# Two levels of the chunked attention in one burst of strip matmuls, with the queries of every other level copied by GpSimd

## The reference

```python
proj = h @ w_in
u, q, zf, zb, iv, g = jnp.split(proj, cuts, axis=-1)
k = (1.0 - lb) * jax.nn.sigmoid(-z)                  # for zf and zb
logf = jnp.logaddexp(jnp.log(lb), jnp.log1p(-lb) + jax.nn.log_sigmoid(z))
...
def step(state, inp):                                # one chunk
    b = jnp.cumsum(gb, axis=2)
    decay = jnp.exp(jnp.where(causal_in_chunk, b_t - b_s, -jnp.inf))
    scores = jnp.einsum("bhtd,bhsd,bhtsd->bhts", qb, kb, decay)
    o = einsum("bhts,bhsv->bhtv", scores, vb) + einsum("bhtd,bhdv->bhtv", qb * exp(b), state)
    state = exp(b_last)[..., None] * state + einsum("bhsd,bhsv->bhdv", kb * exp(b_last - b), vb)
...
y_rec = rms_norm(o_fwd + o_bwd, out_norm) * silu(g)
out = concat([y_fourier, y_rec]) @ w_out             # then experts: router, 16 experts, norm
```

## Time and profile before

| what | value |
|---|---|
| median of 3 runs (lowest, highest) | 2554.42 us (2551.23, 2557.26) |
| the profiled execution's own time | 2552.32 us |
| its span, first to last instruction | 2550.6 us |
| PE busy, share of the span | 98% |
| DVE, ACT, POOL busy | 65%, 53%, 13% |
| granted TensorE clock, mean | 0.997 |
| strips of line 851 | 96 bursts, 32 records each |

### The profile page before, as it was taken

One profiled execution on the slowest core, in us unless ns is written; L12 is line 12 of the kernel. 1 busy time (PEld: TensorE's weight loads), 2 busy tenths in 40 slices (PEclk: granted clock), 3 DMA queues, 4 the chain that ended last, 5 costly groups with the idle time before them and its releaser, 6 DMA issues.

```text
span 2550.6 us, 44352 instructions
## 1 busy us (share of the span) xinstructions
PE 2510.8 (98%) x18109; PEld 2263.5 (89%) x18109; DVE 1648.6 (65%) x1997; ACT 1359.3 (53%) x1627; POOL 327.1 (13%) x237
## 2 busy tenths in 40 slices
PE   7999999999999999999999999999999999999998
PEld 6777778787877999999999999999999999999997
DVE  6556565444387676767667676766767666676667
ACT  6435353434665555555555555555555555555556
POOL 3102020101120011020211202021020202102020
PEclk9999999999999999999999999999999999999999
DMA  4001010135447676675767767676676767667677
GB/s 159 26 22 55 2 55 10 57 137 198 173 144 273 231 256 239 228 261 211 268 228 251 247 235 251 226 259 234 251 249 235 248 221 256 236 234 258 225 259 282
DMA packets 63987, 503.08 MB, mean 197 GB/s; under 512 B 7536, under 2 KB 7920, under 8 KB 39568
## 3 DMA queue, kind: packets, MB, share of 16 engines
q1 hardware_dynamic: 48016, 448.84, 48.3%
q0 software_dynamic: 15872, 52.83, 7.0%
HBM read 464.42 MB, written 37.22 MB: 197 GB/s over the span
## 4 chain that ended last, share of the span: by engine, by line
PE 92%; DVE 3%; ACT 2%; DMA 1%; issue 1%; POOL 0%; SPq 0%; DVEq 0%; ACTq 0%; POOLq 0%
PE up_banks_b L2241 15%; PE up_banks_a L2241 15%; PE up_banks_b L2244 6%; PE up_banks_a L2244 6%; PE bank L64 5%; PE bank L66 5%; PE bank L65 5%; PE up_banks_b L2282 2%; PE up_banks_b L2280 2%; PE up_banks_b L2281 2%; PE up_banks_b L2279 2%; PE up_banks_a L2283 2%; PE up_banks_b L2283 2%; PE up_banks_a L2279 2%; PE up_banks_a L2282 2%; PE up_banks_a L2280 2%
## 5 line engine op out<-in xcount | busy, mean ns | idle before, releaser
L2009 DVE TENSOR_TENSOR big_lo<-wide,big_hi 128x4096 fp32r<-128x4096 f32 x189 | 836.3, 4425 | 410.2 <-ACT big_hi L1774 410.0
L1774 ACT CAST big_hi<-wide 128x4096 fp32r<-128x4096 f32 x190 | 690.3, 3633 | 515.8 <-PE up_banks_a L2241 240.8
L2241 PE MATMUL up_banks_b<-x_parts,big_hi 128*128 128x384 f32 x2016 | 574.3, 356 | 0.0
L2241 PE MATMUL up_banks_a<-x_parts,big_hi 128*128 128x384 f32 x1984 | 565.0, 356 | 1.0 <-DVE h_parts L2033 1.0
L2244 PE MATMUL up_banks_b<-x_parts,big_lo 128*128 128x192 f32 x1764 | 442.0, 251 | 0.0
L2244 PE MATMUL up_banks_a<-x_parts,big_lo 128*128 128x192 f32 x1736 | 435.0, 251 | 0.0
L2241 PEld LDWEIGHTS up_banks_b<-x_parts,big_hi 128*128 128x128 f32 x2016 | 365.3, 189 | 0.2
L2241 PEld LDWEIGHTS up_banks_a<-x_parts,big_hi 128*128 128x128 f32 x1984 | 359.4, 189 | 1.9 <-DVE h_parts L2033 1.2
L2244 PEld LDWEIGHTS up_banks_b<-x_parts,big_lo 128*128 128x128 f32 x1764 | 336.1, 191 | 0.0
L2244 PEld LDWEIGHTS up_banks_a<-x_parts,big_lo 128*128 128x128 f32 x1736 | 330.8, 191 | 0.6
L64 PE MATMUL bank<-big_hi,w_hi 128*128 128x512 f32 x576 | 236.5, 411 | 0.0
(11 more groups left out here) (345 smaller groups left out, 4177.9 us busy)
## 6 DMA issues: line engine op xcount, KB each, us to landing
wide<-in_expert_weights SPq DMA_DIRECT2D x190, 2048.0 KB, 7.7
w_raw<-in_w_heads SPq DMA_DIRECT2D x48, 256.0 KB, 2.8
x_in<-in_x SPq DMA_DIRECT2D x12, 512.0 KB, 4.0
x_d<-in_x POOLq DMA_DIRECT2D x12, 512.0 KB, 5.8
residual<-x_d POOLq DMA_DIRECT2D x12, 512.0 KB, 3.6
ffn_in<-h_and_xT_d POOLq DMA_DIRECT2D x12, 512.0 KB, 3.0
wide<-residual SPq DMA_DIRECT2D x12, 512.0 KB, 6.4
tab<-in_tables POOLq DMA_DIRECT2D x10, 512.0 KB, 7.3
```

The costliest lines, as they stand in the source:

```text
L1774: nc.scalar.copy(ahead.hi(c), raw[:, c % RAW]).then_inc(hi_done, 1)
L2009: nc.vector.tensor_tensor(ahead.lo(c), raw[:, c % RAW], ahead.hi(c).bitcast(F32), ALU.subtract).then_inc(lo_done, 1)
L2241: last = nc.tensor.matmul(out[:, 0:2 * CAP], hi, x[:, k], start=n == 0, stop=n == KT - 1, skip_group_check=True)
```

## The change

1. Levels are done in pairs. Slot s = 1, 3, 5 and 7 has levels s - 1 and s one after the other on TensorE; slots 0, 2, 4 and 6 have none. A block has four bursts of two levels in place of eight of one.
2. A pair needs two sets of keys at once and, as `kq` moves on to the odd level before the pair starts, a copy of the even level's queries. ScalarE copies the keys of both levels (`keys0`, `keys1`), GpSimd copies the queries of levels 2, 4 and 6 into `queries`. A new event `prep` marks where. The functions `prepared` and `unused` hold the waits.
3. VectorE's work on a level is split into `rise` (the decays) and `take_level` (the scores). The rise of an even level waits for the copies of that level (`prepared`), because they read `kq` as it was.
4. ScalarE's copy of `near` into `scores` becomes an event `near` in slot 6.
5. GpSimd's subtractions stand in the order of the timeline, each pair of them at its projection, between the copies of the queries. The first ten still stand at the head.
6. The ring for GpSimd's DMA descriptors (`dynamic_dma_scratch_size`) is 8192 bytes in a partition.

```diff
             for s in range(8):
-                if n < NN:
-                    timeline.append(("level", n, s))
+                if n < NN and s % 2 == 0:
+                    timeline.append(("prep", n, s + 1))
+                    if s == LEVELS - 1:
+                        timeline.append(("near", n))
+                elif n < NN:
+                    timeline += [("level", n, s - 1), ("level", n, s)]
+                    if s < LEVELS:
+                        timeline.append(("prep", n, s + 1))
...
+        def prepared(eng, n, s):
+            copies = LEVELS + LEVELS // 2
+            eng.wait_ge(keys_ready, n * copies + s + s // 2)
...
+        def unused(eng, n, s):
+            if s == 1:
+                eng.wait_ge(kq_made, n + 1)
+            else:
+                eng.wait_ge(kq_up, n * LEVELS + s - 1)
+            if n >= 1 or s > 2:
+                filled(eng, ("level", n, s - 2) if s > 2 else ("level", n - 1, LEVELS + 1 - s))
...
         @block.gpsimd
         def _(pool):
-            for m in range(W_HALVES):
+            for m in range(FIRST_HEAD):
                 weights.low(pool, m)
...
+            for ev in timeline:
+                if ev[0] == "proj":
...
+                    if n % NB == NB - 1 and 2 * ((n // NB + 1) * NJ + g) < W_HALVES:
+                        for f in range(2):
+                            weights.low(pool, 2 * ((n // NB + 1) * NJ + g) + f)
...
+                elif ev[0] == "prep" and ev[2] % 2 == 0:
+                    _, n, s = ev
+                    unused(pool, n, s)
+                    half = 1 << (s - 1)
+                    nc.gpsimd.tensor_copy(queries[:].rearrange("p (n two h) -> p n two h", two=2, h=half),
+                                          halves(n % NB, QB, QF, s - 1, 0, BLK)).then_inc(keys_ready, 1)
...
+                elif kind == "prep":
+                    _, n, s = ev
+                    unused(act, n, s)
+                    half = 1 << (s - 1)
+                    nc.scalar.copy(keys[s % 2][:].rearrange("p (n two h) -> p n two h", two=2, h=half),
+                                   halves(n % NB, KF, KB, s - 1, 0, BLK)).then_inc(keys_ready, 1)
...
-                elif kind == "level" and ev[2] >= 1:
+                elif kind == "level" and ev[2] % 2 == 1:
                     _, n, s = ev
...
+                    rise(n, s)
+                    for t in (s - 1, s):
+                        take_level(("level", n, t))
+                elif kind == "prep" and ev[2] % 2 == 1 and ev[2] > 1:
+                    rise(ev[1], ev[2] - 1)
...
-    nc = bacc.Bacc("TRN2", target_bir_lowering=False, num_devices=1)
+    nc = bacc.Bacc("TRN2", target_bir_lowering=False, num_devices=1, dynamic_dma_scratch_size=8192)
```

More of the change, by code:

```diff
@@ L281, in heads_phase @@
         k_sum = sb("k_sum", [P, BLK])
-        keys = sb("keys", [P, BLK])
+        keys = [sb(f"keys{i}", [P, BLK]) for i in range(2)]
+        queries = sb("queries", [P, BLK])
         sig = sb("sig", [P, 2, BLK])
@@ L512, in split_weights @@
                         weights.high(act, (h * NJ + j) * 2 + f)
[L514 to L524, removed]
             def take_projection(ev):
@@ L581, in _ @@
                     nc.scalar.copy(near[:], near_view[i]).then_inc(bank_read[i], 1)
-                    gather_keys(n, 0)
-                elif kind == "level" and ev[2] < LEVELS:
[L584 to L595, removed]
+                elif kind == "level" and ev[2] == NEAR + 1:
+                    filled(act, ev)
+                    i = fill_of[ev][0]
+                    for j, keys_of in enumerate(STRIPS):
+                        other = STRIPS[j ^ 1]
+                        copied = nc.scalar.copy(scores[keys_of, :, other], bank[i][keys_of, :, other])
+                    copied.then_inc(bank_read[i], 1)
+                elif kind == "level" and ev[2] < LEVELS:
+                    continue
                 elif kind == "level":
@@ L647, in sig_in, with rise, take_level @@
                 return sig[:, i % 2], sig_used[i % 2]
+            def rise(n, s):
+                nonlocal own
+                b, level = n % NB, s - 1
+                half = 1 << level
+                if level == 0:
+                    dve.wait_ge(kq_made, n + 1)
+                else:
+                    dve.wait_ge(kq_up, n * LEVELS + level)
+                pair = "p r (n two h) -> p r n two h"
+                products = decay[level][:].rearrange("p r (n two) -> p r n two", two=2)
+                shape = [P, 2, BLK // (2 * half), half]
+                right = kq[b][:, QF:KB + 1].rearrange(pair, two=2, h=half)[:, :, :, 1]
+                left = kq[b][:, KF:QB + 1].rearrange(pair, two=2, h=half)[:, :, :, 0]
+                up = decay[level + 1][:] if level + 1 < LEVELS else chunk_decay[:, b]
+                own += 1
+                nc.vector.tensor_tensor(up, products[:, :, :, 0], products[:, :, :, 1], ALU.mult).then_inc(dve_step, 1)
+                if s % 2 == 1:
+                    filled(dve, ("level", n, s))
+                else:
+                    prepared(dve, n, s)
+                own += 1
+                nc.vector.tensor_tensor(right, right, products[:, :, :, 0].unsqueeze(3).to_broadcast(shape), ALU.mult)\
+                    .then_inc(dve_step, 1)
+                nc.vector.tensor_tensor(left, left, products[:, :, :, 1].unsqueeze(3).to_broadcast(shape), ALU.mult)\
+                    .then_inc(kq_up, 1)
+            def take_level(ev):
+                _, n, s = ev
+                i = fill_of[ev][0]
+                if 1 <= s <= NEAR:
+                    filled(dve, ev)
+                    was_read(dve, ("level", n, s - 1))
+                    nc.vector.copy_predicated(near[:], mask[:, s - 1].unsqueeze(1).to_broadcast([P, CH, STRIP]),
+                                              near_view[i]).then_inc(bank_read[i], 1)
+                elif s == LEVELS:
+                    filled(dve, ev)
+                    dve.wait_ge(intra_done, n)
+                    nc.vector.tensor_copy(scores[P // 2:, :, 0:P // 2], bank[i][P // 2:, :, 0:P // 2])\
+                        .then_inc(bank_read[i], 1)
             norm.vector(dve)
@@ L832, in _ @@
                     else:
-                        pe.wait_ge(keys_ready, n * LEVELS + s)
+                        prepared(pe, n, s)
                     for c in range(CH):
```

61 lines of the change are left out of this document (21 added, 40 removed).

## The result

| | median us (lowest, highest) | runs |
|---|---|---|
| before | 2553.20 (2550.93, 2557.26) | 17 |
| changed | 2558.12 (2556.00, 2560.72) | 17 |

The ratio is 1.0021, 95% interval 1.0014 to 1.0027: slower by 4.9 us, where -1.9 us were forecast. The profiled span went from 2550.6 to 2555.3 us, at the same mean clock of 0.997. The heads stage holds most of it: the first matmul after the heads starts at 556.19 us before and at 560.27 us after, 4.1 us later; the remaining 0.6 us of the span come behind the heads and were not followed up. The time lies inside the range given for 8 in 10 (2544 to 2563 us) and just outside the forecast's own (2549 to 2558), but the sign is the other one.

A forecast was written before the change was run, and what follows sets the result against it. TensorE's own order was taken as the bound (busy 37.80 of 38.10 us in one block). The terms -9.0 - 0.9 + 0.3 + 7.3 + 0.4 = -1.9 us gave 2552.5 us, with 2544 to 2563 us for 8 in 10.

The forecast's parts named there:

- Part 1, the bursts: TensorE's strip bursts: merging levels saves 0.31 us per joined level, with level 0's move -9.0 us in all.
- the 0.9 us that the prediction named as a sign of being wrong: TensorE's pairs of levels: a pair costing more than 0.9 us would show the prediction wrong.
- Leaving level 0's old place: Between transposed keys and state products: moving level 0 away gains 0.1 us a block, 1.2 us in all.
- Part 2: an ordinary pair: Ordinary windows: next pair ready at 5.8 us, TensorE free at 6.4, slack hides the chain; 0.3 us for contention.
- between slots 5 and 7 nothing can be late: Slots 5 to 7: TensorE has four halves, 11 us, so no lateness was counted.
- Part 3: Blocks 1, 4, 7 and 10: GpSimd's subtractions delay copies and VectorE, costing 7.3 us, between 3.4 and 16.
- two state copies at 3.95: Block 4, slots 1 to 3: VectorE's masked copy ends at 3.55 us, its two state copies at 3.95.
- outer bound of 2.6: Block 4, slots 1 to 3: the loss if both state updates and the queries' copy are late, 2.6 us.
- GpSimd gets in first and the chain is late: Rival, slots 1 and 3 of blocks 1, 4, 7, 10: stalls of 16 us, time 2562.6 us; chance 0.15.
- VectorE always first: Rival: VectorE gets in before GpSimd's subtractions, part 3 only 3.4 us, time 2548 us; chance 0.33.
- slow copy: Rival: GpSimd's copy of the queries takes 3 us, costing +26 us, time 2579 us; chance 0.06.
- unshared entry: Rival: two levels of a TensorE burst don't share their entry, +13 us, time 2567 us; chance 0.04.

The follow-up runs named there:

- one-column kernels: GpSimd's subtractions for later heads' weights cut to one column: in the changed kernel 2546.1 us, ratio 0.997; in the kernel before 2552.47 us, ratio 0.9998.
- experiment 4: Changed kernel with ScalarE's copy of level 0 into near ahead of the sigmoid of slot 0: 2556.44 us, ratio 1.0014 to the kernel before.
- experiment 6: Changed kernel with only GpSimd's two V subtractions moved behind the seventh rise of the block: 2556.0 us, ratio 1.0014 to the kernel before.

## Why the prediction was wrong

**Part 1, the bursts: right in mechanism, somewhat too large.** A pair of two plain levels (2 and 3, or 4 and 5) costs 1.35 - 0.46 = 0.89 us of TensorE's time, for 0.87 taken. The pairs with level 1 and with level 7 cost 0.96 and 1.07 us, over the 0.9 us that the prediction named as a sign of being wrong; but the bursts of levels 1 and 7 cost more before, too (0.67 and 0.78 us alone, for 0.59). Like for like, each level that joins another saves 0.29 to 0.30 us where 0.31 was taken. That it came so close is partly luck: the row for the price of more passes has passes of 16 columns, and a strip's have 32. Blocks 2, 5 and 8 became 0.65 us shorter, where 0.75 were forecast. Leaving level 0's old place gave the 0.1 us at the ends of blocks 2, 5 and 8 alone: block 5 goes from transposed keys to state products in 1.20 us (290.29 to 291.49) where it took 1.30, with the 0.22 us wait for `k_tok` that was foreseen. In the other blocks this stretch is as long as before, so the term was worth some 0.3 us for the 1.2 counted.

Without the subtractions, blocks 1 to 11 gain 6.0 us (one-column kernels, 416.4 to 410.3 us), with block 0 7.2. The forecast for the same was 9.9 - 0.3 - 0.4 = 9.2. Most of the missing 2.0 us is in blocks 4, 7 and 10, which gained 0.31 to 0.35 us each where 1.05 was forecast (0.75, and the wait of 0.3 us that goes). Their first product with a state still starts 4.07 us behind the pair (216.52 to 220.59 us), with a wait of 0.29 us; in block 3 it is 3.63 us, and with ScalarE's copy of level 0 first (experiment 4, block 4) again 3.63. So this part is ScalarE's late copy and not GpSimd.

**Part 2: an ordinary pair has the slack that was worked out.** No strip in blocks 2, 3, 5, 6, 8 or 9 waited for keys. In block 5 the second rise ends 5.02 us behind the pair's start (260.48 to 265.50 us), for 5.05 forecast, and the next pair comes at 6.43. The copy on GpSimd takes 0.63 us (22.7 us for 36), less than the 0.8 taken:

```profile
L528 POOL COPY queries<-kq 128x512 f32<-128x512 f32 x36 | 22.7, 632 | 227.2 <-DVE kq L703 220.7 <-DMA fnet_u<-sig 6.5
```

Block 11 did wait, in the way and at the place that were forecast: GpSimd's copy stands behind the store of `u`, and level 3 starts 0.50 us behind level 2 in place of 0.28.

```profile
496.37 0.67 POOL L528 COPY queries<-kq 128x512 f32<-128x512 f32 x1 [2.51 <-DMA fnet_u<-sig]
...
498.41 0.62 ACT L601 COPY keys<-kq 128x512 f32<-128x512 f32 x1 [3.29 <-DVE kq L703]
498.67 0.46 PE L900 MATMUL bank<-queries,keys 128*32 128x32 f32 x32
499.17 0.46 PE L900 MATMUL bank<-kq,keys 128*32 128x32 f32 x32
```

It cost some 0.2 us, for 0.4 taken.

What failed here is the sentence that between slots 5 and 7 nothing can be late. It counted projections ahead of the pair of levels 6 and 7 and nothing behind it. Blocks 3, 6 and 9 have the V subtractions right at that pair, with the scaling of the outputs, its transposition on TensorE and `intra` queued on VectorE after it. Cost: 0.93 x 3 = 2.8 us, forecast 0. This is the first failing step, and experiment 6 gets the 0.93 us back by moving those subtractions alone.

**Part 3: the place was right and the size was not.** The stalls came in blocks 1, 4, 7 and 10, at the states in slot 2 and the keys of slot 5, where they were forecast, but 9.8 us in all for 7.3 (changed against one-column), and near 12 counted from no wait at all, as the forecast counted, since 0.7 us in each of blocks 4, 7 and 10 stay in the one-column kernel (in the sum below they are in its gain of 6.0). The step that was mis-sized is "two state copies at 3.95". It priced them at their usual length, because the updates in the earlier trace rows have two SBUF inputs and I took that for the condition. The copies have one, and took 1.68 us. The steps ahead of them came as worked out: ScalarE's copy of level 0 ended 3.24 us behind the pair (forecast 3.3) and the masked copy 3.64 (3.55), but the state copies 5.22 (3.95). Hence 2.0 us at the states for the 1.1 taken, within the outer bound of 2.6; slots 3 to 5 lost 1.05 for 0.8, since a subtraction got ahead of the left halves by 0.08 us, which the forecast had the other way round. The wait for keys in slot 3 did not appear, because the stall at the states had already covered it; experiment 4 brought it out, 0.94 us. This is the second failing step. The row of block 1 in the trace before, 2.25 us for two copies, would have shown it.

The Trainium skill (SBUF — State Buffer, Who interferes with whom), the section that the prediction cites for two inputs, also lists copies among the instructions that can take the pair of ports shared with GpSimd, if their operands meet certain conditions; who comes second then waits for the other's whole instruction. That sentence was not weighed. The trace agrees: two plain copies took 0.36 us alone and 1.68 us beside a subtraction.

**The sum by measured terms:** block 0 -1.2, blocks 1 to 11 without subtractions -6.0, blocks 1, 4, 7 and 10 +9.8, blocks 3, 6 and 9 +2.8, less the 0.6 us that block 1 lost to GpSimd before already: +4.8 us. The forecast had -9.2, +7.3 and 0 for these, -1.9. The profiled span changed by 4.7 us; that this is so near is because two things outside the terms cancel, 0.7 us less in the input stage and 0.6 us more behind the heads.

**Rivals.** "GpSimd gets in first and the chain is late" was the nearest, with 2562.6 us for all eight windows. It was given 0.15; the rows gave more reason for it than that, for the prediction itself said that GpSimd asks right after its roundings. "VectorE always first" (0.33) is refuted: its row was two updates, of which the first began 0.25 us before the subtraction and the second waited (1.69 us for both, 0.60 alone), so it was no evidence that an instruction which asks later gets in first. The slow copy and the unshared entry are refuted by 0.63 and 0.28 us. (The price of the slow copy counted ten ordinary windows; eight blocks have two each, 16.)

## What to carry to other kernels

Where GpSimd and VectorE both work in SBUF, write down the order of their starts, not only their durations: a shift of 0.3 us turned left halves of 0.68 us into 1.78 to 1.80 us nine times, where none had been slow before, and here whoever started second paid the rest of the other's instruction. Merging bursts is a shift of everything behind them, so each meeting that was won by less than the shift has to be counted anew, also in slots that seem to have time. Before an instruction is moved out of another's way, look at what its end releases: here it was a load buffer, and the stall came back through a third engine.

## What the runs showed that was not expected

- A copy of 128x128 float32 from SBUF to SBUF on VectorE waits for a GpSimd subtraction as an instruction with two SBUF inputs does: 1.68 us for two (2.25 us in block 1 before), 0.36 us alone. The masked copy, which reads PSUM, kept its 0.31 us inside the same subtraction (223.26 us).
- Two subtractions of 128x512 on GpSimd take 2.52 us beside the state copies in block 4 and 3.02 us where VectorE's products of 128x512 stand between them: both sides pay.
- GpSimd copies 128x512 float32 in 0.63 us, as fast as ScalarE (0.62 to 0.69), half of its subtraction.
- The 8 KB ring changed nothing that 11 runs can tell (within 0.1%).
